# The second head group's softmax: sink column written on a change of head only, and the maxima of two score blocks taken by one instruction

## The reference

```python
def window_attention(q, k, v, sink):
    ...
    s = jnp.einsum('bnqkgd,bnckd->bnkgqc', qb, kb).astype(jnp.float32) * scale
    ...
    s = jnp.where(valid[None, :, None, None], s, -jnp.inf)
    sink_l = sink.astype(jnp.float32).reshape(1, 1, Hkv, G, 1, 1)
    m = jnp.maximum(jnp.max(s, axis=-1, keepdims=True), sink_l)
    e = jnp.exp(s - m)
    den = jnp.sum(e, axis=-1, keepdims=True) + jnp.exp(sink_l - m)
    p = (e / den).astype(v.dtype)
    o = jnp.einsum('bnkgqc,bnckd->bqnkgd', p, vb)
```

## Time and profile before

| | |
|---|---|
| median of 3 runs | 1337.9 us (1337.68 to 1338.1) |
| profiled execution | span 1336.2 us, from its first to its last instruction |
| PE matmul busy | 1321.8 us, 99% |
| DVE busy | 657.8 us, 49% |
| ACT busy | 537.7 us, 40% |
| attention, group B steps | from about 126.6 us (first mask matmul) to 178.8 us |

### The profile page before, as it was taken

The page is one execution under the profiler, slowest core; times in us unless marked ns, Lnnn a source line. Parts: engine busy times, 40 slices in busy tenths (PEclk is TensorE's granted clock), DMA queues, the critical chain, the costliest instruction groups (busy, mean ns, idle before and its releaser), DMA issues.

```text
span 1336.2 us, 14846 instructions
## 1 busy us (share of the span) xinstructions
PE 1321.8 (99%) x6184; PEld 1062.0 (79%) x6184; DVE 657.8 (49%) x907; ACT 537.7 (40%) x732; POOL 93.4 (7%) x95
## 2 busy tenths in 40 slices
PE   9999999999999999999999999999999999999998
PEld 7864568788888888887888888888888888888887
DVE  4887663755353531227434555563644443423246
ACT  6568654533232322234225556533423232322235
POOL 0000004300000000003000001011000000000103
PEclk9999999999999999999999999999999999999999
DMA  7200013122222223242221111222222222223321
GB/s 300 107 32 1 1 63 127 64 95 95 95 95 95 85 87 108 87 136 75 101 95 63 64 63 64 94 95 95 95 95 95 95 95 95 82 91 96 109 95 64
DMA packets 21170, 119.85 MB, mean 90 GB/s; under 512 B 2544, under 2 KB 2928, under 8 KB 10480
## 3 DMA queue, kind: packets, MB, share of 16 engines
q1 hardware_dynamic: 20400, 118.20, 25.3%
q10 hardware_dynamic: 704, 0.70, 0.2%
HBM read 116.80 MB, written 2.10 MB: 89 GB/s over the span
## 4 chain that ended last, share of the span: by engine, by line
PE 94%; DVE 3%; ACT 1%; DMA 1%; issue 1%; SPq 0%; DVEq 0%; ACTq 0%
PE ps L504 92%; PE ps L751 2%; DMA w_raw<-weights 1%; DVE w_lo L1445 1%; DVE prob L1449 0%; ACT prob L995 0%; DVE nmax L1663 0%; ACT w_hi L995 0%; DVE rt L1452 0%; DVE hf L1452 0%; SPq L443 0%; PE ps L585 0%; SPq L439 0%; DVE X L1445 0%; DVE h_lo L1445 0%
## 5 line engine op out<-in xcount | busy, mean ns | idle before, releaser
L504 PE MATMUL ps<-h_hi,w_hi 128*128 128x512 f32 (+1 forms) x1256 | 491.8, 392 | 1.6 <-DVE w_lo L1445 0.9
L504 PE MATMUL ps<-h_hi,w_lo 128*128 128x512 f32 (+1 forms) x1256 | 487.4, 388 | 0.0
L504 PE MATMUL ps<-h_lo,w_hi 128*128 128x512 f32 (+1 forms) x1256 | 487.4, 388 | 0.0
L1445 DVE TENSOR_TENSOR w_lo<-w_raw,w_hi 128x2048 fp32r<-128x2048 f32 (+2 forms) x117 | 240.9, 2062 | 273.2 <-ACT w_hi L995 273.2
L995 ACT ACTIVATE w_hi<-w_raw 128x2048 fp32r<-128x2048 f32 (+2 forms) x117 | 201.3, 1722 | 201.2 <-DMA w_raw<-weights 201.1
L504 PEld LDWEIGHTS ps<-h_hi,w_hi 128*128 128x128 f32 x1256 | 235.8, 188 | 56.8 <-issue 6.1
L504 PEld LDWEIGHTS ps<-h_hi,w_lo 128*128 128x128 f32 x1256 | 235.8, 188 | 48.7
L504 PEld LDWEIGHTS ps<-h_lo,w_hi 128*128 128x128 f32 x1256 | 235.9, 188 | 48.6 <-issue 1.0
L504 PE MATMUL ps<-mid_hi,w_hi 128*128 128x512 f32 x352 | 136.9, 389 | 0.0
L504 PE MATMUL ps<-mid_lo,w_hi 128*128 128x512 f32 x352 | 136.9, 389 | 0.0
L504 PE MATMUL ps<-mid_hi,w_lo 128*128 128x512 f32 x352 | 136.9, 389 | 0.0
(11 more groups left out here) (193 smaller groups left out, 1097.0 us busy)
## 6 DMA issues: line engine op xcount, KB each, us to landing
w_raw<-weights SPq DMA_DIRECT2D x81, 1024.0 KB, 4.9
w_raw<-weights SPq DMA_DIRECT2D x32, 704.0 KB, 4.2
PT<-x SPq DMA_DIRECT2D x4, 512.0 KB, 15.8
out<-OUT SPq DMA_DIRECT2D x8, 256.0 KB, 2.5
X<-x_t SPq DMA_DIRECT2D x3, 512.0 KB, 7.1
c<-constants SPq DMA_DIRECT2D x1, 1280.0 KB, 11.8
w_raw<-weights SPq DMA_DIRECT2D x4, 256.0 KB, 6.8
wp_raw<-weights SPq DMA_DIRECT2D x1, 1024.0 KB, 6.9
```

Of the source, the lines that this page charges most:

```text
L504: return nc.tensor.matmul(out, lhsT, rhs, start=start, stop=stop, skip_group_check=loose)
L1445: return nc.vector.tensor_tensor(out, a, b, op)
```

## The change

The reductions of group B are issued once for two steps, at the even one, over both banks (2 x 257 or 2 x 385 columns into two columns of `nmax`), and release both. The sink column is written only for steps with b = 0 and 1; the steps with b = 2 and 3 of the same head find it in the bank from before. PE's wait counts the columns accordingly. The change holds for steps 32 to 63; group A is as before.

```diff
@@ scores(t), PE
                 if kind:
-                    pe.wait_ge(sink_ready, 2 * (t - 16) + 2)
+                    pe.wait_ge(sink_ready, 4 * c + 2 * min(b, 1) + 2)
@@ negmax(s), DVE
                 kind, h, b, k0, k1 = STEPS[s]
+                if kind and s % 2:
+                    return
                 dve.wait_ge(s_done, s // 2 + 1)
-                at, end = (SINK_AT - (k1 - k0) * P, SINK_AT + 1) if kind else (0, S)
-                nc.vector.tensor_reduce(nmax[:, s:s + 1], ps[:, s % 4, at:end], AX.X, ALU.max,
+                if kind:
+                    at, end = SINK_AT - (k1 - k0) * P, SINK_AT + 1
+                    nc.vector.tensor_reduce(nmax[:, s:s + 2], ps[:, s % 4:s % 4 + 2, at:end], AX.X, ALU.max,
+                                            negate=True).then_inc(nmax_ready, 2)
+                    return
+                nc.vector.tensor_reduce(nmax[:, s:s + 1], ps[:, s % 4, 0:S], AX.X, ALU.max,
                                         negate=True).then_inc(nmax_ready, 1)
@@ the loop over the steps, DVE
                 dve.wait_ge(exp_done, s + 1)
-                if s + 4 < 64 and STEPS[s + 4][0]:
+                if s + 4 < 64 and STEPS[s + 4][0] and STEPS[s + 4][2] < 2:
                     at = G_SINK + STEPS[s + 4][1]
```

## The result

| | before | changed |
|---|---|---|
| median of 6 runs each | 1337.97 us (1337.68 to 1338.23) | 1341.91 us (1341.38 to 1342.06) |
| ratio | | 1.0029, 95% interval 1.0019 to 1.0039 |
| span of the profiled execution | 1336.2 us | 1340.2 us |

The changed kernel is 3.9 us slower. That is the sign and the mechanism forecast, at almost twice the size: 2.2 us was predicted. The time, 1341.91 us, lies at the upper end of the range that the prediction gave (1337.6 to 1341.9), and above the 1338.4 to 1340.5 of its own forecast case.

A forecast was written before the change was run, and what follows sets the result against it. PE was taken to bound the kernel, waiting for DVE's odd-step multiplications; 4.8 us of possible delays, less slacks and credits, left 2.2 us on 1337.9, so 1340.1 us, range 1337.6 to 1341.9.

The forecast's parts named there:

- own forecast case: The delay lands as walked, plus 0.5 to 2.6 us, between 1338.4 and 1340.5 us; chance 0.50.
- What bounds: Group B: PE, busy 99% of the span, waits 4.3 us in 8 waits for DVE's multiplication ahead of transposes.
- The price of the reduction: Two-step reductions on DVE, one fixed part each: 0.95 us for 2 x 385 columns, 0.69 for 2 x 257.
- slower rival: Reduction pays its fixed part per bank (1.11 and 0.84 us), or credits stay out: 4.1 us, 1342.0; chance 0.36 together.
- the sum: Walk over group B's odd steps, adding only delay beyond PE's slack, less credits: PE leaves group B 2.2 us later.
- The credits: Delay given back: 0.12 us at step 43, 0.08 at 55, then from 2.89 at 59 to 2.1 at 62.
- The slacks at 31 to 41: PE's slack at odd steps, 0.21, 0, 0.03, 0.17, 0.12 and 0 us, leaves 1.25 us of delay.
- The sink edit: 16 of 32 sink copies on DVE go, 0.07 us each on the chain; alone worth 0.3 to 0.4 us.
- The pass to the end: Behind group B PE is busy 99% of the time, so the 2.2 us pass in full to the end.
- fewer DVE instructions would pay: Faster rival: every removed DVE instruction shortens the path, 3.7 us gone, 1334.2 us; chance 0.06.
- The case in which gains and delays cancel: Exponentials of odd steps, released earlier, take a wait out of ACT: 1337.9 us, between 1336 and 1338.4; chance 0.08.
- The estimate of 4.0 us: From the skill's 120 cycles at 0.96 GHz per PSUM-source operation: 32 DVE instructions fewer give 4.0 us, time 1333.9.

The follow-up runs named there:

- after_busy: The changed kernel with five extra unread matmuls on PE after the transposes of steps 48, 50, 52, 56 and 58; 1341.7 us.
- two_rows_a: The changed kernel with each 128x512 maximum of group A taken as two rows of 256 in one bank; 1341.64 us (one run).
- after_shift: The changed kernel with six tiny DVE memsets just ahead of the first attention step; 1341.16 us (one run).
- late_singles: The kernel before with the sink edit, both single-step maxima of a pair issued behind the odd step's multiplication; 1336.16 us, ratio 0.9987.
- late_pair: The changed kernel with its two-step reduction issued behind the odd step's multiplication instead of ahead of it; 1338.71 us, ratio 1.0007.
- two_singles: The kernel before with the sink edit, both maxima of a pair issued at the even step as two instructions; 1341.22 us, ratio 1.0025.

## Why the prediction was right in sign and short in size

**What bounds.** Right. PE's wait for the odd multiplication decides: PE's idle time in the last stretch grew from 3.25 to 5.0 us as DVE's work shrank, and moving the maxima to the other side of that multiplication, with single reductions in both cases, turned 3.3 us of loss into 1.8 of gain. DVE was idle for the exponentials of the odd steps 43, 55 and 61 before; in the changed kernel it is for none of an odd step, as the prediction said.

**The price of the reduction.** Right to 0.01 us: 0.959 and 0.693. The slower rival's mechanism, a fixed part for each bank, would have been 1.11 us and is refuted, though the time came out next to the one it gave (1342.0). That the measured time still lies in the range is luck in part: the range was wide enough for this rival, and what filled it was a wait, a late start and a clock that nobody had in the sum.

**The wait on the reduction.** This is the term that the sum lacked. The prediction took over the 0.02 us between the scores' end and the maximum from the earlier trace rows without asking whether the new instruction would carry its wait as the old did. It did not, and 0.07 us came on in every round. For the eleven odd steps of 31 to 41, 43, and 47 to 53 that is 0.77 of the 0.97 us by which step 53 is later than walked. Over some 14 rounds it is 1.0 us.

**The credits.** Mostly as walked. From step 53 to 55 the shift fell by 0.02 (0.08 less the new 0.07). From 59 to 62 it fell by 0.61, where 0.8 was walked; the rest went to the low clock, for with the clock at 1.00 it fell by 0.79 in after_busy and two_rows_a and by 0.80 in after_shift. At step 43, the walk had PE's delay fall by 0.12; it stayed (1.79 after 1.77), 0.07 of that being the wait.

**The slacks at 31 to 41** were read nearly rightly: 1.25 walked and six times 0.07 is 1.67, measured 1.77.

**What was not on the list.** The one late reduction (0.35 us) and the low clock (0.5 us in the profiled execution). The sum is then 2.2 + 1.0 + 0.35 + 0.5 = 4.05 of 4.38 us. The 0.3 us that are left stand at three places: 0.10 by step 41, 0.07 at step 43, and about 0.15 between step 62 and the first projection matmul, where 0.1 was walked and after_busy and after_shift, at full clock, show 0.25. Their reasons stay open.

**The sink edit.** Right: 0.3 us by the trace; the medians differ by 0.5, which the interval does not tell from nothing.

**The pass to the end.** Right: the first projection matmul is 4.0 us later on the clock of the trace (182.83 to 186.84), and the span 4.0.

**The rivals.** That fewer DVE instructions would pay (the rule of the Trainium skill's "VectorE: DVE Perf Modes", section "Rules for kernel authors", to keep the number of operations small) did not hold here: DVE's busy time fell by 1.7 us and the kernel lost 3.9. It did not hold with the order put right either, since late_singles, with 16 more reductions than late_pair, is 2.6 us faster. The case in which gains and delays cancel did not come either. The exponentials gave nothing to set against the delay: ACT's waits for the maxima grew (3.0 us in 4 waits before, 6.6 in 8 after). The estimate of 4.0 us from the cycle table of the Trainium skill's "VectorE: DVE Perf Modes", section "The TRN2 errata — SBUF-src ops pay a fixed extra latency per instruction", also counted the 16 sink copies, which read SBUF, as PSUM sources, and its fixed part of 0.125 us is below the 0.16 of the earlier trace rows.

## What to carry to other kernels

When two instructions of an in-order engine are merged, ask first what stood between them: here it was the one instruction that the busiest engine waits for, and the merge put 0.4 us ahead of it to save 0.06. Then ask who waits for the first half, as the exponential did. The same question, put to the kernel before, finds the better order: what PE waits for goes first, what has slack goes behind it. And a merged instruction whose semaphore count changes may no longer carry its own wait, which a count of all instructions in the page gives away.

## What the runs showed of the hardware

- Where DVE was idle at a wait that is an instruction of its own (21 ns in the trace), the next instruction started 0.06 to 0.08 us after it in 56 of 60 cases in the kernel before, and in fifteen of sixteen at the two-step reductions of the changed one. For the two-step reductions that made 0.11 to 0.12 us after the matmuls' end in place of 0.04 to 0.05. Where DVE was busy (late_pair) the wait cost nothing.
- A maximum over two rows costs as one over their sum of columns, in one bank (0.687 us for 2 x 256, 0.652 for 2 x 240) or two (0.959 for 2 x 385, 1.224 for 2 x 512).
- When such a separate wait stood at place 319, 447 or 575 of DVE's list and DVE was idle, the next instruction started 0.42 us after it, 0.35 late, in each trace that has one there, with the kernel before among them. Six instructions added ahead of it took the delay away, and so did a wait carried by the instruction itself (two_singles at place 319).
- The granted clock fell from 1.00 to 0.50 for 3.4 us after PE had idled 1.65 us in one gap, in three profiles, and not in a fourth with the same gap. It did not fall in after_busy, where extra matmuls left 0.54 us of that gap. It cost 0.5 us.
